# Stick-breaking attention on one Trainium2 core: far mask added by VectorE, off-diagonal sums shortened, value matmuls of two heads interleaved

## The chip, the cores and the metric

The kernel is one program on one core of a Trainium2 chip. It computes two transformer blocks in one launch, over 512 positions of width 1024, in float32 throughout. The metric is the device time of that launch in microseconds (us). The change touches one stage of it, the attention of the last layer.

## The reference, cut to what matters

The last attention is a stick-breaking attention with 16 heads of 64 over 512 positions, causal and strict:

```python
z = einsum('bqhd,bkhd->bhqk', qb, kb) * scale
strict = tk[None, :] < tq[:, None]
log_fail = where(strict, log_sigmoid(-z), 0.0)
between = cumsum(log_fail, axis=-1, reverse=True) - log_fail
a = where(strict, exp(log_sigmoid(z) + between), 0.0)
out = einsum('bhqk,bkhd->bqhd', a, vb)
```

`log_sigmoid(-z)` is minus softplus(z), so the exponent of a pair (query t, key s) is z minus the sum of softplus(z) over the keys from s to t. The masked pairs get a large negative number added to z (the far mask), which makes both softplus and the exponential vanish.

## The kernel before

Scores are kept transposed: keys on the 128 partitions, queries along the free axis. There are four key tiles `kt` of 128, and key tile `kt` needs queries from `kt * 128` on, so it has 512, 384, 256 and 128 columns. Together that is `SB_W` = 1280 columns in three PSUM banks. `SB_AT` says where each tile starts; tiles 0 and 2 begin banks of their own, and tile 3 (at 896) lies behind tile 1 in the second bank. The first 128 columns of each tile are its diagonal block, the only place where the far mask is needed. Two heads alternate between PSUM banks 0 to 2 and 3 to 5; the value outputs of a pair of heads share bank 6 or 7, one head on partitions 0 to 63 and one on 64 to 127.

For each head `h`, in four engines' programs that only semaphores tie together:

- TensorE, `scores(h)`: four matmuls with 64 rows (L1241), 1280 columns in all, then four matmuls of the identity with `k.far` (L1244), 128 columns each, which add the far mask to the diagonal blocks. It may start when the exponential of head `h - 2` has been read out of the same banks (`a.exped`).
- ScalarE: Abs (L1287) of the scores, Exp (L1289), a table load and Ln (L1291), which gives log(1 + exp(-|z|)).
- VectorE (L1309): max(z, 0) plus that, the softplus `k.sp`, 1280 wide. It waits for Ln, and for the sums of the head before.
- TensorE, `sums(h)` (L1254): ten matmuls that subtract the running sums from z in PSUM. Four have `minus_later` (a triangle) as weights and 1280 columns in all; six have `minus_ones` and add the key tiles further on, another 1280 columns.
- ScalarE (L1296): a table load and Exp of the result into `k.tt`.
- TensorE, `values(h)` (L1264): four matmuls with 64 output columns of the array, 1280 columns in all. ScalarE copies the outputs of a pair out (L1300).

The loop is one head deep: in turn `h`, TensorE's order is `scores(h)`, `sums(h - 1)`, `values(h - 2)`, and ScalarE's is Abs, Exp, Ln of `h`, then Exp of `h - 1`, then in odd turns the copy of a pair. Each engine runs its program strictly in that order. After the last head the output projection (L233) follows, then routing and the experts. A float32 matmul instruction leaves two records in the trace, so four of them show as x8.

Of the kernel before, what the change touches and what calls it, by code (L numbers as in the profile page):

```python
# [5 lines left out]
ALU = mybir.AluOpType  # L6
# [15 lines left out]
HEAD = 64  # L22
# [13 lines left out]
DIFF_HEADS, SB_HEADS = 8, 16  # L36
# [24 lines left out]
class Chain:  # L61
# [1159 lines left out]
SB_AT = (0, 512, 1024, 896)  # L1221
# [3 lines left out]
def sb_cols(kt, frm=None):  # L1225

    frm = kt if frm is None else frm
    return slice(SB_AT[kt] + (frm - kt) * P, SB_AT[kt] + (TT - kt) * P)


def sb_scores(k, h):
    return k.ps[:, 3 * (h % 2):3 * (h % 2) + 3, :].rearrange("p b n -> p (b n)")


def sb_tensor(pe, k, a):
    def scores(h):
        if h >= 2:
            pe.wait_ge(a.exped, h - 1)
        r = slice(h % 2 * HEAD, (h % 2 + 1) * HEAD)
        for kt in range(TT):  # L1240
            pe.matmul(sb_scores(k, h)[:, sb_cols(kt)], k.k[r, h // 2, kt * P:(kt + 1) * P],  # L1241
                      k.q[r, h // 2, kt * P:T], start=(kt < TT - 1), stop=False, skip_group_check=True)
        for kt in range(TT):
            mm = pe.matmul(sb_scores(k, h)[:, SB_AT[kt]:SB_AT[kt] + P], k.ident[:, :], k.far,  # L1244
                           start=False, stop=True, skip_group_check=True)
        mm.then_inc(a.scored, 1)

    def sums(h):

        pe.wait_ge(a.softplus, h + 1)  # L1250
        for kt in range(TT):
            for st in range(kt, TT):
                lhs = k.minus_later if st == kt else k.minus_ones
                mm = pe.matmul(sb_scores(k, h)[:, sb_cols(kt, st)], lhs, k.sp[:, sb_cols(st)],  # L1254
                               start=False, stop=True, skip_group_check=True)
        mm.then_inc(a.summed, 1)

    def values(h):
        pe.wait_ge(a.exped, h + 1)
        if h % 2 == 0 and h >= 4:  # L1260
            pe.wait_ge(a.oT_out, h // 2 - 1)
        out = k.ps[h % 2 * HEAD:(h % 2 + 1) * HEAD, 6 + h // 2 % 2, :]
        for kt in range(TT):
            mm = pe.matmul(out[:, kt * P:T], k.v[:, kt, h * HEAD:(h + 1) * HEAD], k.tt[:, h % 2, sb_cols(kt)],  # L1264
                           start=(kt == 0), stop=(kt == TT - 1))
        mm.then_inc(a.valued, 1)

    pe.wait_ge(a.proj_act, QKV_JOBS // 2)
    pe.wait_ge(a.proj_dve, QKV_JOBS // 2)
    for h in range(SB_HEADS + 2):  # L1270
        if h < SB_HEADS:
            scores(h)
        if 1 <= h <= SB_HEADS:
            sums(h - 1)
        if h >= 2:
            values(h - 2)
    pe.wait_ge(a.oT_out, SB_HEADS // 2)


def sb_scalar(act, k, a):  # L1280
    for h in range(SB_HEADS + 2):
        if h < SB_HEADS:

            act.wait_ge(a.scored, h + 1)
            if h:
                act.wait_ge(a.softplus, h)
            act.activation(k.ln[:, :], sb_scores(k, h)[:, 0:SB_W], ACT.Abs).then_inc(a.steps, 1)  # L1287
            act.wait_ge(a.steps, 2 * h + 1)
            act.activation(k.ln[:, :], k.ln[:, :], ACT.Exp, scale=-1.0).then_inc(a.steps, 1)  # L1289
            act.wait_ge(a.steps, 2 * h + 2)  # L1290
            act.activation(k.ln[:, :], k.ln[:, :], ACT.Ln, bias=k.one_col, scale=1.0).then_inc(a.logged, 1)  # L1291
        if 1 <= h <= SB_HEADS:
            act.wait_ge(a.summed, h)
            if h >= 3:
                act.wait_ge(a.valued, h - 2)
            act.activation(k.tt[:, (h - 1) % 2, :], sb_scores(k, h - 1)[:, 0:SB_W], ACT.Exp).then_inc(a.exped, 1)  # L1296
        if h >= 3 and h % 2 == 1:
            pair = (h - 3) // 2
            act.wait_ge(a.valued, 2 * pair + 2)
            act.copy(k.oT[:, pair, :], k.ps[:, 6 + pair % 2, :]).then_inc(a.oT_out, 1)  # L1300


def sb_vector(dve, k, a):

    for h in range(SB_HEADS):
        dve.wait_ge(a.logged, h + 1)
        if h:
            dve.wait_ge(a.summed, h)
        dve.scalar_tensor_tensor(out=k.sp[:, :], in0=sb_scores(k, h)[:, 0:SB_W], scalar=0.0, in1=k.ln[:, :],  # L1309
                                 op0=ALU.max, op1=ALU.add).then_inc(a.softplus, 1)  # L1310

# [407 lines left out]
def place(k, nc, ctx):  # L1719
# [76 lines left out]
    k.dist_i = at(12800, T).bitcast(I32)  # L1796
    k.nmax, k.esum, k.hsmall = at(17408, 2, 4), at(17416, 2, 5), at(17426, 4, TT)
    k.gate_diff, k.gate_diff_b, k.tmp_diff = at(0, D), at(D, D), at(12800, 2, 512)
    k.ln, k.sp, k.tt = at(12288, SB_W), at(13568, SB_W), at(14848, 2, SB_W)
    k.minus_ones, k.minus_later, k.far = at(17408, P), at(17536, P), at(17664, P)  # L1800
    k.gate_sb, k.gate_sb_b, k.tmp_sb = at(12288, D), at(13568, D), at(14848, 2, 512)
# [28 lines left out]
def semaphores(nc, prefix, names):  # L1830
    return [nc.alloc_semaphore(name=prefix + n) for n in names.split()]
# [186 lines left out]
def second_block_layer(nc, k, w, out, l):  # L2018

    s, a, m = Kit(), Kit(), Kit()  # L2020
# [7 lines left out]
    if l == 0:  # L2028
        (a.biased, a.maxed, a.weighed, a.turned, a.turned_out, a.squared, a.var, a.rooted, a.head_normed, a.head_turned) = semaphores(
            nc, "diff_", """biased maxed weighed turned turned_out squared var rooted head_normed head_turned""")  # L2030
    else:
        (a.steps, a.logged, a.softplus, a.summed) = semaphores(
            nc, "sb_", """steps logged softplus summed""")
    k.used[("diff", "sb")[l]] = {"proj": a.proj, "out": a.out}
    (m.router_landed, m.logits, m.g_diff, m.e_diff, m.exps, m.chosen, m.ranked, m.routed, m.scattered, m.x_landed,
     m.x_turned, m.xT_act, m.xT_dve, m.gate_landed, m.up_landed, m.down_landed, m.gated, m.upped, m.downed, m.hidden,
# [22 lines left out]
    with nc.Block() as block:  # L2059
# [151 lines left out]
```

## Time and profile before

| what | us |
| --- | --- |
| median of three runs | 2960.25 |
| the three runs | 2954.14, 2960.25, 2967.46 |
| span of the profiled execution | 2963.8 |
| TensorE matmul busy | 2409.4 (81%) |
| ScalarE busy | 619.3 (21%) |
| VectorE busy | 534.1 (18%) |
| last attention, first scores to the output projection | 2083.4 to 2279.5 |

The profiled execution lies 3.55 us above the median of the runs. The last attention is 196 us of it, 6.6% of the span; there the shares are different from those of the whole, so the rows below are read from that stretch. A timeline row gives the start, the length and the engine of one instruction or a merged group, and in brackets how long the engine sat idle before it and what it then waited for.

### The profile page before, as it was taken

To read this page: it belongs to the slowest core of one execution; us is meant where nothing else is said; L and a number is where in the kernel's file an instruction comes from. 1 tells how busy PE (TensorE), PEld (TensorE's weight loads), DVE (VectorE), ACT (ScalarE), POOL (GpSimd) and SP (SyncE) were. 2 spreads that over 40 slices of the span, in tenths; PEclk is the share of its full clock that TensorE was granted. 3 is DMA by queue.
4 is the path that set the end of the run, shared out by engine and by line. 5 is a ranking of instruction groups with operands and counts; after the bars stand their busy time and mean duration, and the time that the engine had idled before them with its cause. 6 is when DMAs were issued, how large, how long until landed. Compare 5 with 4: busy or idle time off the path is not lost. (4 is left out here: it accounts for less than half of the span.)

```text
span 2963.8 us, 21879 instructions
## 1 busy us (share of the span) xinstructions
PE 2409.4 (81%) x8560; PEld 1103.4 (37%) x8560; DVE 534.1 (18%) x1147; ACT 619.3 (21%) x937; POOL 131.9 (4%) x205
## 2 busy tenths in 40 slices
PE   6988899999997996764888878399899748878773
PEld 3443444444443444441223222244555422222221
DVE  1223532121002016431010010300111211010012
ACT  2213421010001016311121121200564102121121
POOL 2101101000000000001000000100000010000001
PEclk9999789999998998876989999699999868999996
DMA  6245756602221101016999999610200149999994
GB/s 232 72 148 198 254 199 231 253 20 75 103 85 57 57 38 76 15 59 248 427 428 429 428 427 429 256 57 0 114 0 15 59 172 428 428 427 429 428 427 197
DMA packets 126889, 624.34 MB, mean 211 GB/s; under 512 B 13708, under 2 KB 17172, under 8 KB 102252
## 3 DMA queue, kind: packets, MB, share of 16 engines
q1 hardware_dynamic: 102224, 556.35, 46.5%
q0 software_dynamic: 13392, 49.61, 4.5%
q10 hardware_dynamic: 11212, 17.52, 1.6%
q8 instruction: 42, 0.69, 0.1%
q14 instruction: 19, 0.16, 0.0%
HBM read 570.99 MB, written 52.48 MB: 210 GB/s over the span
## 5 line engine op out<-in xcount | busy, mean ns | idle before, releaser
L226 PE MATMUL ps<-hT,ring 128*128 128x512 f32 (+1 forms) x1424 | 619.5, 597 | 9.0 <-DVE hT L181 4.7
L1487 PE MATMUL ps<-ring,arena 128*64 128x512 f32 x2048 | 516.4, 666 | 133.6 <-ACT arena L1515 115.5
L226 PEld LDWEIGHTS ps<-hT,ring 128*128 128x128 f32 (+1 forms) x1424 | 270.3, 190 | 356.4 <-issue 351.8
L1487 PEld LDWEIGHTS ps<-ring,arena 128*64 128x64 f32 x2048 | 160.5, 153 | 467.8 <-issue 385.0
L233 PE MATMUL ps<-ring,hT 128*128 128x512 f32 x640 | 278.6, 596 | 1.5 <-ACT hT L1160 0.8
L1502 PE MATMUL ps<-ring,arena 128*64 128x512 f32 x1024 | 238.7, 620 | 31.3 <-ACT arena L1522 31.3
L233 PEld LDWEIGHTS ps<-ring,hT 128*128 128x128 f32 x640 | 121.8, 191 | 156.9 <-issue 154.8
L948 PE MATMUL ps<-ring,arena 128*128 128x512 f32 x336 | 144.4, 592 | 0.8 <-issue 0.8
L1502 PEld LDWEIGHTS ps<-ring,arena 128*64 128x64 f32 x1024 | 83.0, 142 | 164.9 <-issue 128.1
L1545 DVE TENSOR_TENSOR arena<-ps,arena 128x512 f32<-128x512 f32 x32 | 22.1, 692 | 603.5 <-PE ps L1487 603.5
L189 PE MATMUL ps<-ident,arena 128*128 128x128 f32 x192 | 34.9, 366 | 92.6 <-DVE arena L177 92.6
L948 PEld LDWEIGHTS ps<-ring,arena 128*128 128x128 f32 x336 | 63.8, 190 | 81.5 <-issue 81.5
L1477 PE MATMUL ps<-ident,arena 128*128 128x128 f32 x256 | 38.7, 296 | 66.1 <-DMA arena<-token_slots 66.1
L1254 PE MATMUL ps<-arena 128*128 128x128 f32 (+3 forms) x320 | 79.1, 405 | 4.7 <-DVE arena L1309 4.7
L1044 ACT ACTIVATE arena<-ps 128x512 f32<-128x512 f32 x24 | 14.3, 597 | 307.0 <-PE ps L226 201.9
L1548 DVE COPY arena<-ps 128x512 f32<-128x512 f32 x32 | 22.1, 692 | 300.1 <-PE ps L1502 300.1
L1522 ACT COPY arena<-ps 128x512 f32<-128x512 f32 x32 | 18.8, 586 | 270.6 <-PE ps L1492 270.6
L1050 DVE TENSOR_SCALAR arena<-ps 128x512 f32<-128x512 f32 x24 | 16.6, 691 | 318.5 <-PE ps L226 214.2
L1520 ACT ACTIVATE arena<-ps 128x512 f32<-128x512 f32 x32 | 19.1, 597 | 257.8 <-PE ps L1487 257.8
L1525 ACT COPY arena<-ps 128x512 f32<-128x512 f32 x32 | 18.8, 586 | 254.0 <-PE ps L1502 254.0
L189 PEld LDWEIGHTS ps<-ident,arena 128*128 128x128 f32 x192 | 33.8, 214 | 96.8 <-DVE arena L177 91.8
L971 ACT COPY arena<-ps 128x512 f32<-128x512 f32 x21 | 12.3, 587 | 259.0 <-PE ps L226 259.0
(329 smaller groups left out, 2060.3 us busy)
## 6 DMA issues: line engine op xcount, KB each, us to landing
ring<-in_expert_w_gate SPq DMA_DIRECT2D x64, 2048.0 KB, 16.6
ring<-in_expert_w_down SPq DMA_DIRECT2D x64, 2048.0 KB, 19.7
ring<-in_expert_w_up SPq DMA_DIRECT2D x64, 2048.0 KB, 19.6
ring<-in_ada_w SPq DMA_DIRECT2D x24, 2048.0 KB, 12.9
arena<-token_slots SPq DMA_DIRECT2D x32, 512.0 KB, 22.8
output_slots<-arena ACTq DMA_DIRECT2D x32, 512.0 KB, 10.2
token_slots<-arena POOLq DMA_DIRECT2D x1, 12288.0 KB, 40.5
output_slots<-arena POOLq DMA_DIRECT2D x1, 12288.0 KB, 77.5
```

The source lines that it names most:

```text
L189: mm = pe.transpose(k.ps[:, c, tt * P:(tt + 1) * P], k.xn[:, tt, c::KD], k.ident[:, :])
L226: mm = pe.matmul(out, w[:, c, cols], x[:, c, :], start=(c == 0), stop=(c == chunks - 1))
L233: mm = pe.matmul(out, x[:, c, tt * P:(tt + 1) * P], w[:, c, :], start=(c == 0), stop=(c == chunks - 1))
L948: mm = pe.matmul(k.ps[:, 4 * half + tt, :], k.actT[:, c0 + c, tt * P:(tt + 1) * P], w[:, c, :], start=(c0 + c == 0), stop=(c0 + c == FT - 1))
L1254: mm = pe.matmul(sb_scores(k, h)[:, sb_cols(kt, st)], lhs, k.sp[:, sb_cols(st)], start=False, stop=True, skip_group_check=True)
L1477: mm = pe.transpose(k.ps[:, c // 4, c % 4 * P:(c % 4 + 1) * P], k.xg[:, c::KD], k.ident[:, :])
L1487: mm = pe.matmul(k.ps[slots, 2 + kind, :], k.xT[:, c, slots], w[:, c, :], start=(c == 0), stop=(c == KD - 1))
L1502: mm = pe.matmul(k.ps[slots, 5 + half, :], k.hTt[:, c, slots], w[:, c, half * 512:(half + 1) * 512], start=(c == 0), stop=(c == KH - 1))
L1520: act.activation(k.sg[:, :], k.ps[:, 2, :], ACT.Silu).then_inc(m.silu, 1)
L1522: act.copy(k.hTt[:, :, :].rearrange("p c s -> p (c s)"), k.ps[:, 4, :]).then_inc(m.hT_out, 1)
L1545: dve.tensor_tensor(k.hid[:, :], k.ps[:, 3, :], k.sg[:, :], ALU.mult).then_inc(m.hidden, 1)
L1548: dve.tensor_copy(k.ys[:, 512:1024], k.ps[:, 6, :]).then_inc(m.y_dve, 1)
```

## The change

Three things change in the attention of the last layer.

1. The four identity matmuls that added the far mask are gone. VectorE adds it in PSUM with two instructions for each head (`mark(h)`: three blocks of 128 in one, then the last block). ScalarE's Abs now waits for these (`a.marked`). `mark(h + 1)` stands behind the softplus of head `h` in VectorE's program.
2. `sums` has nine matmuls in place of ten and 2048 columns in place of 2560: VectorE first adds off-diagonal tiles of `k.sp` into `k.spc` (three additions of 128 columns each), and the last two matmuls read that, behind a wait for `a.carried`.
3. `values` is called once for a pair of heads, with the matmuls of the two heads alternating, and stands ahead of `sums` in odd turns; even turns have none.

```diff
         for kt in range(TT):
-            for st in range(kt, TT):
-                lhs = k.minus_later if st == kt else k.minus_ones
-                mm = pe.matmul(sb_scores(k, h)[:, sb_cols(kt, st)], lhs, k.sp[:, sb_cols(st)],
-                               start=False, stop=True, skip_group_check=True)
-        mm.then_inc(a.summed, 1)
+            pe.matmul(z[:, sb_cols(kt)], k.minus_later, k.sp[:, sb_cols(kt)], start=False, stop=True, skip_group_check=True)
+        for kt in range(TT - 1):
+            pe.matmul(z[:, sb_block(kt, kt + 1)], k.minus_ones, k.sp[:, sb_block(kt + 1, kt + 1)],
+                      start=False, stop=True, skip_group_check=True)
+        pe.wait_ge(a.carried, 3 * h + 3)
+        pe.matmul(z[:, sb_block(0, 2, 2)], k.minus_ones, k.spc[:, 0:2 * P], start=False, stop=True, skip_group_check=True)
+        pe.matmul(z[:, sb_block(1, 3)], k.minus_ones, k.spc[:, 2 * P:3 * P], start=False, stop=True, skip_group_check=True)\
+            .then_inc(a.summed, 1)
...
+    def values(pair):
+        pe.wait_ge(a.exped, 2 * pair + 2)
+        if pair >= 2:
+            pe.wait_ge(a.oT_out, pair - 1)
         for kt in range(TT):
-            mm = pe.matmul(out[:, kt * P:T], k.v[:, kt, h * HEAD:(h + 1) * HEAD], k.tt[:, h % 2, sb_cols(kt)],
-                           start=(kt == 0), stop=(kt == TT - 1))
+            for n in range(2):
+                h = 2 * pair + n
+                mm = pe.matmul(k.ps[n * HEAD:(n + 1) * HEAD, 6 + pair % 2, kt * P:T], k.v[:, kt, h * HEAD:(h + 1) * HEAD],
+                               k.tt[:, n, sb_cols(kt)], start=(kt == 0), stop=(kt == TT - 1))
...
+    def mark(h):
+        dve.wait_ge(a.scored, h + 1)
+        diagonal = k.ps[:, 3 * (h % 2):3 * (h % 2) + 3, 0:P]
+        dve.tensor_tensor(diagonal, diagonal, k.far.unsqueeze(1).to_broadcast([P, TT - 1, P]), ALU.add).then_inc(a.marked, 1)
+        last = sb_scores(k, h)[:, sb_block(TT - 1, TT - 1)]
+        dve.tensor_tensor(last, last, k.far, ALU.add).then_inc(a.marked, 1)
...
+        dve.wait_ge(a.softplus, h + 1)
+        dve.tensor_tensor(k.spc[:, 2 * P:3 * P], k.sp[:, sb_block(2, 3)], k.sp[:, sb_block(3, 3)], ALU.add).then_inc(a.carried, 1)
+        dve.tensor_tensor(k.spc[:, 0:P], k.sp[:, sb_block(1, 2)], k.sp[:, sb_block(2, 2)], ALU.add).then_inc(a.carried, 1)
+        dve.wait_ge(a.carried, 3 * h + 1)
+        dve.tensor_tensor(k.spc[:, P:2 * P], k.sp[:, sb_block(1, 3)], k.spc[:, 2 * P:3 * P], ALU.add).then_inc(a.carried, 1)
+        if h + 1 < SB_HEADS:
+            mark(h + 1)
```

On TensorE, before, one turn of the steady loop (the mask matmuls L1244, the ten sums L1254, the values of one head L1264, the next scores L1241) reads so:

```order
L1244 MATMUL ps<-arena,ident 128x128 x4
L1254 MATMUL ps<-arena 128x512
L1254 MATMUL ps<-arena 128x384
L1254 MATMUL ps<-arena 128x256
L1254 MATMUL ps<-arena 128x128
...
L1264 MATMUL ps<-arena 64x512
L1264 MATMUL ps<-arena 64x384
L1264 MATMUL ps<-arena 64x256
L1264 MATMUL ps<-arena 64x128
L1241 MATMUL ps<-arena 128x512
```

On TensorE, of the changed kernel, an odd turn from the end of its scores (L1246) to the start of the next, even turn: L1271 is the values of a pair, L1255 and L1257 the sums from `k.sp`, L1260 and L1261 those from `k.spc`.

```order
L1246 MATMUL ps<-arena 128x128
L1271 MATMUL ps<-arena 64x512 x2
L1271 MATMUL ps<-arena 64x384 x2
L1271 MATMUL ps<-arena 64x256 x2
L1271 MATMUL ps<-arena 64x128 x2
L1255 MATMUL ps<-arena 128x512
L1255 MATMUL ps<-arena 128x384
L1255 MATMUL ps<-arena 128x256
L1255 MATMUL ps<-arena 128x128
L1257 MATMUL ps<-arena 128x128 x3
L1260 MATMUL ps<-normw,arena 128x256
L1261 MATMUL ps<-normw,arena 128x128
```

The mask matmuls have left the queue, the values moved from behind the sums to ahead of them, and in the even turn that follows nothing stands between the scores and the sums, nor behind the sums until the next scores.

On VectorE, before, the whole stage is one kind of instruction (L1309, the softplus), between the last copies of the projections (L1050) and the output projection's products and sums:

```order
L1050 TENSOR_SCALAR arena<-ps 128x512 x12
L1309 SCALAR_TENSOR_TENSOR arena<-ps,arena 128x1280 x16
L1069 TENSOR_TENSOR arena<-ps,arena 128x512
L1071 TENSOR_TENSOR x<-x,arena 128x512
L1069 TENSOR_TENSOR arena<-ps,arena 128x512
```

On VectorE, of the changed kernel, the first heads of the stage read so (L1315 and L1317 are `mark`, L1325 the softplus, L1328, L1329 and L1331 the additions into `k.spc`):

```order
L1315 TENSOR_TENSOR ps<-ps,arena 128x3x128
L1317 TENSOR_TENSOR ps<-ps,arena 128x128
L1325 SCALAR_TENSOR_TENSOR arena<-ps,arena 128x1280
L1328 TENSOR_TENSOR normw<-arena 128x128
L1329 TENSOR_TENSOR normw<-arena 128x128
L1331 TENSOR_TENSOR normw<-arena,normw 128x128
L1315 TENSOR_TENSOR ps<-ps,arena 128x3x128
L1317 TENSOR_TENSOR ps<-ps,arena 128x128
L1325 SCALAR_TENSOR_TENSOR arena<-ps,arena 128x1280
```

The mask of head 0 comes ahead of its softplus; from then on the mask of head `h + 1`, for which Abs of that head waits, stands behind the softplus and the three additions of head `h`.

ScalarE's instructions and their order are unchanged but for what they wait for.

## Rows read from the trace of the kernel before

**Rows 1.** Stage by windows: length, then busy us (instructions) per engine, granted clock, DMA share, GB/s.

```profile
2083.00:2280.00 197.00, 176.33 (x705) 114.97 (x706) 24.15 (x17) 128.06 (x105) 1.17 (x2) 0.92 0.12 48
```

**Rows 2.** Waits in 14 turns of the loop: us in total, times, longest.

```profile
ACT arena L1287 <- PE ps L1244: 54.6, 14, 5.1
PE ps L1241 <- ACT arena L1296: 14.9, 13, 1.9
```

**Rows 3.** Timeline of one turn at the full clock: start, us, engine, what.

```profile
2180.25 4.50 PE L1254 MATMUL ps<-arena 128*128 128x512 f32 x20
...
2180.45 1.24 ACT L1287 ACTIVATE arena<-ps 128x1280 f32<-128x1280 f32 x1 [2.85 <-PE ps L1244]
...
2184.68 2.37 PE L1264 MATMUL ps<-arena 128*64 128x512 f32 x8
...
2185.69 1.49 DVE L1309 SCALAR_TENSOR_TENSOR arena<-ps,arena 128x1280 f32<-128x1280 f32 x1 [9.42 <-ACT arena L1291]
...
2186.97 1.24 ACT L1296 ACTIVATE arena<-ps 128x1280 f32<-128x1280 f32 x1
...
2188.26 2.42 PE L1241 MATMUL ps<-arena 64*128 64x512 f32 x8 [1.22 <-ACT arena L1296]
...
2190.61 1.16 PE L1244 MATMUL ps<-arena,ident 128*128 128x128 f32 x8
...
2191.81 1.24 ACT L1287 ACTIVATE arena<-ps 128x1280 f32<-128x1280 f32 x1 [3.60 <-PE ps L1244]
```

**Rows 4.** Timeline of a turn at the low clock, and windows around such a fall.

```profile
2163.53 2.97 PE L1241 MATMUL ps<-arena 64*128 64x512 f32 x8 [1.22 <-ACT arena L1296]
...
2168.30 6.38 PE L1254 MATMUL ps<-arena 128*128 128x512 f32 x20
...
2115.00:2117.00 2.00, 1.48 (x4) 0.86 (x5) 0.00 (x0) 0.47 (x1) 0.00 (x0) 1.00 0.00 0
2117.00:2119.00 2.00, 2.00 (x8) 1.52 (x7) 0.00 (x0) 0.00 (x0) 0.00 (x0) 0.62 0.00 0
```

**Rows 5.** Timeline, ScalarE: Abs of heads 2 and 15.

```profile
2107.71 1.24 ACT L1287 ACTIVATE arena<-ps 128x1280 f32<-128x1280 f32 x1 [3.60 <-PE ps L1244]
...
2263.27 1.24 ACT L1287 ACTIVATE arena<-ps 128x1280 f32<-128x1280 f32 x1 [4.65 <-PE ps L1244]
```

**Rows 6.** Timeline and window of the first two heads.

```profile
2095.02 7.24 PE L1254 MATMUL ps<-arena 128*128 128x512 f32 x20 [4.67 <-DVE arena L1309]
...
2095.07 1.24 ACT L1287 ACTIVATE arena<-ps 128x1280 f32<-128x1280 f32 x1 [1.62 <-DVE arena L1309]
...
2104.16 2.42 PE L1241 MATMUL ps<-arena 64*128 64x512 f32 x8 [1.90 <-ACT arena L1296]
...
2095.00:2097.00 2.00, 1.98 (x3) 0.95 (x4) 0.00 (x0) 1.92 (x2) 0.00 (x0) 0.50 1.01 434
```

**Rows 7.** The first attention: TensorE timeline and windows.

```profile
1141.39 0.90 PE L1099 MATMUL ps<-ident,arena 128*128 128x128 f32 x3 [5.49 <-DVE arena L1189]
...
1138.00:1140.00 2.00, 0.00 (x0) 0.00 (x0) 1.97 (x7) 0.98 (x1) 0.00 (x0) 0.50 0.00 0
1142.00:1144.00 2.00, 2.00 (x12) 1.67 (x10) 1.38 (x4) 1.25 (x5) 0.00 (x0) 0.50 0.00 0
```

**Rows 8.** Timeline, TensorE: expert matmuls on half the columns alternating; projection matmuls.

```profile
1417.55 7.09 PE L1502 MATMUL ps<-ring,arena 128*64 128x512 f32 x32 [0.68 <-ACT arena L1522]
...
999.68 12.61 PE L226 MATMUL ps<-hT,ring 128*128 128x512 f32 x29
```

**Rows 9.** Groups by line and form, VectorE: busy us, mean ns, idle before.

```profile
L1545 DVE TENSOR_TENSOR arena<-ps,arena 128x512 f32<-128x512 f32 x32 | 22.1, 692 | 603.5 <-PE ps L1487 603.5
...
L1347 DVE TENSOR_TENSOR arena<-arena 128x128 f32<-128x128 f32 x4 | 1.2, 292 | 0.1
```

**Rows 10.** Timeline of the end of the stage.

```profile
2274.89 3.93 PE L1264 MATMUL ps<-arena 128*64 128x512 f32 x16
...
2279.49 20.87 PE L233 MATMUL ps<-ring,hT 128*128 128x512 f32 x48 [0.68 <-ACT hT L1300]
```

More of the change, by code:

```diff
@@ L1228, in sb_cols, with sb_block @@
     return slice(SB_AT[kt] + (frm - kt) * P, SB_AT[kt] + (TT - kt) * P)
+def sb_block(kt, q, n=1):
+    return slice(SB_AT[kt] + (q - kt) * P, SB_AT[kt] + (q - kt + n) * P)
 def sb_scores(k, h):
@@ L1240, in scores @@
         for kt in range(TT):
[L1241 to L1244, printed above, removed]
-                           start=False, stop=True, skip_group_check=True)
+            mm = pe.matmul(sb_scores(k, h)[:, sb_cols(kt)], k.k[r, h // 2, kt * P:(kt + 1) * P],
+                           k.q[r, h // 2, kt * P:T], start=(kt < TT - 1), stop=True, skip_group_check=True)
         mm.then_inc(a.scored, 1)
@@ L1250, in sums @@
         pe.wait_ge(a.softplus, h + 1)
+        z = sb_scores(k, h)
         for kt in range(TT):
-            for st in range(kt, TT):
-                lhs = k.minus_later if st == kt else k.minus_ones
-                mm = pe.matmul(sb_scores(k, h)[:, sb_cols(kt, st)], lhs, k.sp[:, sb_cols(st)],
-                               start=False, stop=True, skip_group_check=True)
-        mm.then_inc(a.summed, 1)
[L1258 to L1262, printed above, removed]
+            pe.matmul(z[:, sb_cols(kt)], k.minus_later, k.sp[:, sb_cols(kt)], start=False, stop=True, skip_group_check=True)
[10 more added lines that the diff above has]
+            pe.wait_ge(a.oT_out, pair - 1)
         for kt in range(TT):
-            mm = pe.matmul(out[:, kt * P:T], k.v[:, kt, h * HEAD:(h + 1) * HEAD], k.tt[:, h % 2, sb_cols(kt)],
-                           start=(kt == 0), stop=(kt == TT - 1))
+            for n in range(2):
+                h = 2 * pair + n
+                mm = pe.matmul(k.ps[n * HEAD:(n + 1) * HEAD, 6 + pair % 2, kt * P:T], k.v[:, kt, h * HEAD:(h + 1) * HEAD],
+                               k.tt[:, n, sb_cols(kt)], start=(kt == 0), stop=(kt == TT - 1))
         mm.then_inc(a.valued, 1)
@@ L1272, in sb_tensor @@
             scores(h)
+        if h >= 3 and h % 2:
+            values((h - 3) // 2)
         if 1 <= h <= SB_HEADS:
             sums(h - 1)
-        if h >= 2:
-            values(h - 2)
     pe.wait_ge(a.oT_out, SB_HEADS // 2)
@@ L1282, in sb_scalar @@
         if h < SB_HEADS:
-            act.wait_ge(a.scored, h + 1)
+            act.wait_ge(a.marked, 2 * h + 2)
             if h:
@@ L1294, in sb_scalar @@
             if h >= 3:
-                act.wait_ge(a.valued, h - 2)
+                act.wait_ge(a.valued, (h - 1) // 2)
             act.activation(k.tt[:, (h - 1) % 2, :], sb_scores(k, h - 1)[:, 0:SB_W], ACT.Exp).then_inc(a.exped, 1)
@@ L1298, in sb_scalar @@
             pair = (h - 3) // 2
-            act.wait_ge(a.valued, 2 * pair + 2)
+            act.wait_ge(a.valued, pair + 1)
             act.copy(k.oT[:, pair, :], k.ps[:, 6 + pair % 2, :]).then_inc(a.oT_out, 1)
 def sb_vector(dve, k, a):
+    def mark(h):
[4 more added lines that the diff above has]
+        dve.tensor_tensor(last, last, k.far, ALU.add).then_inc(a.marked, 1)
+    dve.wait_ge(k.s.later_ready, 2)
+    mark(0)
     for h in range(SB_HEADS):
@@ L1798, in place @@
     k.gate_diff, k.gate_diff_b, k.tmp_diff = at(0, D), at(D, D), at(12800, 2, 512)
+    k.spc = k.normw[:, 0:3 * P]
     k.ln, k.sp, k.tt = at(12288, SB_W), at(13568, SB_W), at(14848, 2, SB_W)
@@ L2031, in second_block_layer @@
     else:
-        (a.steps, a.logged, a.softplus, a.summed) = semaphores(
-            nc, "sb_", """steps logged softplus summed""")
+        (a.steps, a.logged, a.softplus, a.marked, a.carried, a.summed) = semaphores(
+            nc, "sb_", """steps logged softplus marked carried summed""")
     k.used[("diff", "sb")[l]] = {"proj": a.proj, "out": a.out}
```

## The prediction

> **What bounds the stage now.** I read the windows of the stage first, then the waits, then the timeline of one turn, because the page's shares are averages over stages with other limits. In the stage [rows 1] TensorE is busy 176 of 197 us, ScalarE 128, VectorE 24: that looks like a TensorE bound. The waits say otherwise. In 14 turns Abs waited 54.6 us for the mask matmuls, and the scores waited 13 times, 14.9 us, for ScalarE's last Exp [rows 2]. The two engines form a ring, and the timeline shows it closed [rows 3]: Abs of one head at 2180.45; Abs, Exp, table load, Ln, table load, Exp run on without a gap until 2186.97 + 1.24 = 2188.21, which is 7.76 us; the next scores start 0.05 later, at 2188.26; the mask matmuls follow; the next Abs starts at 2191.81, 3.55 us after the scores. Turn: 11.36 us = 7.76 + 0.05 + 3.55. The sums (4.43 us from 2180.25 to 2184.68) and the values (2.37) run beside ScalarE's 7.76 us. They end 1.22 us before the scores may start, so at the full clock they are hidden.
>
> From Abs of head 2 to Abs of head 15 there are 13 turns in 155.56 us [rows 5], 11.97 each, 0.61 above the full-clock turn. The rest is TensorE's clock. Between 2115 and 2117 TensorE is busy 1.48 of 2 us at a granted clock of 1.00, and in the next 2 us it is at 0.62, though busy all the time; the waits before scores are where the clock falls [rows 4]. Where it falls, the scores and the mask take 4.77 us to the start of the sums (2163.53 to 2168.30), and Abs starts 0.2 after that, so 4.97 in place of 3.55: a turn costs 1.4 more, and somewhat more where sums and values are late too (sums 6.38 in place of 4.50). At 0.61 a turn this happens in about every second one.
>
> **The mask on VectorE (part 1).** Removed from the ring: the mask matmuls, at the full clock 3.55 - 2.42 - 0.04 = 1.09 us of it [rows 3]. Put in their place: one addition over 3 x 128 and one over 128, from PSUM to PSUM, which no row shows. The nearest rows are an addition of 512 from PSUM, 692 ns, and one of 128, 292 ns [rows 9]; the line through them gives 559 for 384. So 0.85, with two hand-overs and a gap 0.95; at worst two of the 512-wide kind, 1.4; at best, if only the streaming counts (400 ns for 384 wider), 0.6. I take 0.95: the ring gets 0.15 shorter, a turn 11.2. VectorE has room: softplus begins 5.24 us after Abs (2185.69), lasts 1.49, the three additions take 3 x 0.3 = 0.9, so it is free 7.65 us after Abs, while the next scores end 10.2 after it. Only in the first turns does the queue matter (below).
>
> **The shorter sums (part 2).** 2048 columns for 2560: 4.43 x 0.8 = 3.55 us. Off the ring at the full clock: worth nothing there by itself. The wait for the additions comes after seven matmuls (about 2.9 us) and the additions take 0.9, so it holds nothing up.
>
> **The values in pairs (part 3).** Alternating matmuls on two halves of the columns run side by side in the expert stage: 32 records of 512 columns in 7.09 us, 0.22 each, against 0.43 each for full-width ones [rows 8]. A pair would take 2.2 us if perfect and 4.5 if not at all; the widths fall from 512 to 128 and each matmul has two records, so I take 2.65. That is hidden too: in an odd turn 2.65 + 3.55 = 6.2 us stand behind the scores, and the Exp that needs the sums comes 0.95 + 6.5 = 7.45 us behind them.
>
> **What TensorE does with the time.** All three parts empty TensorE in a ring whose length hardly changes. It had 1.22 us of idle time a turn. In an even turn it will have 11.2 - 2.35 - 3.55 = 5.3 us in one piece, ahead of the scores on which the ring waits; in an odd turn 11.2 - 2.35 - 6.2 = 2.6 us. What such a gap does stands in two places. Ahead of the first sums TensorE was idle 4.67 us, and it then ran them at a granted clock of 0.50, 1.2 GHz: 7.24 us [rows 6]. In the first attention it was idle 5.49 us; the clock was 0.50 before the gap was over and still 0.50 through 2 us of full work [rows 7]. So the scores of every odd turn run at half clock: their 2.13 us of streaming (1280 columns, at the rate of 0.43 for 512 columns and two records for each matmul) doubles, +2.1 on the ring, or +1.9 where the clock returns within them. The values behind them are slow in part, about +1, and still covered (7.2 against 7.45). In even turns the gap is 2.6 less what the slow turn took, about 2; that is more than the 1.22 after which the clock falls in every second turn now, so I put between half (0.6) and all (1.4) of a fall there: 1.0.
>
> The Trainium skill, page TensorE: Matmul & The Clock Gate, Part 1, says that the default state is throttled and that activity releases the throttle. It speaks against this change. By that rule the sum is the one below; without it the ring alone would give the first rival's time. The rows just named agree with it.
>
> **The sum, against the profiled execution (2963.8 us).**
> Steady turns: an odd one 11.2 + 2.0 = 13.2, an even one 11.2 + 1.0 = 12.2, mean 12.7; 13 x (12.7 - 11.97) = **+9.5**.
> Beginning: Abs of head 1 started at 2095.07, straight after softplus. Now it is behind the three additions and its own mask, 0.9 + 0.95: +1.85, less 0.15 for head 0. The first sums are short, so ahead of the scores of head 2 (2104.16 before, after 1.90 idle [rows 6]) there is a gap of over 4 us, and these scores run slow: +2.1, less 0.15. **+3.6** (+1.6 if the clock stays).
> End: before, 2263.27 to 2279.49, 16.2 us from Abs of head 15 to the output projection [rows 5, 10]. After: Ln ends 5.2 after Abs, softplus 1.5, sums 3.6 with their drain, Exp 1.3, the pair of values 2.8, the copy 0.65, small hand-overs 0.2: 15.25. **-1.0**. At half clock the last of these would cost up to 2 more.
> Together +12.1: 2975.9 for such an execution. The profiled one lies 3.55 above the median of its runs, so **2972 us** for the median. Nothing behind the stage hides this: its weights have landed, and the output projection starts when the last copy is done. The forecast's own spread, from 0.6 to 1.4 for the even turns, 0.6 to 1.4 for the mask and 0 to 2 at the end, is 2964 to 2983.
>
> **Rivals.**
> *The clock holds.* If the idle pieces fall so that it keeps 2.4 GHz, the ring alone counts: 13 x (11.2 - 11.97) = -10, beginning +1.6, end -1: -9.4, 2951. For it: in about half of the turns the clock did hold over an idle piece of over 1 us, and values of two heads at once keep more of the array busy. Against: both rows with gaps of about 5 us. 0.13.
> *Half clock in both turns and late sums.* If an odd turn is slow from scores to sums, these end at 5.1 + 7.1 = 12.2 us behind the scores against 7.45 needed, and Exp is late by 4.7; it decides where the clock stays low for well over 7 us of work after a gap. After the first gap it was low for some 2 x (7.24 - 4.50) = 5.5 us [rows 3, 6]. With the even turns slow as well (+2.1) and one odd turn in three late like this (+1.6 on average) the mean turn is 11.2 + 2.1 + 0.8 = 14.1: 13 x 2.1 = +28, ends +5: 2993. 0.2.
> *The values don't run side by side.* Pairs of unequal records, each matmul's two in a row, may take turns. Then a pair is 4.5 us, 8.05 behind the scores at the full clock, 0.6 late in an odd turn; with half of the values at half clock as well 6.5 + 3.55 = 10.05, 2.6 late. 7 x 2.6 = +18 on the forecast: 2990. 0.04.
> A mask as dear as two 512-wide additions adds 13 x 0.45 = 6 to any of these; the ranges hold it.
>
> **Chances.** Forecast 0.63, clock holds 0.13, half clock throughout 0.2, values apart 0.04. A measurement of this kernel tells about 0.5% (15 us) from no change. The forecast lies 12 above the median with a spread of some 7, so 0.41 of its 0.63 is within that and 0.22 is slower; the clock rival gives 0.03 faster and 0.10 same; the others slower but for 0.01. Sum: faster 0.03, same 0.52, slower 0.45. The range takes the forecast whole, half of the way to the first rival and the second rival with half its weight: 2955 to 2993.
>
> **What would show it.** Right: turns (Abs to Abs) that alternate near 13 and 12 us; over 5 us idle ahead of every second scores, and 0.50 in the windows over them; scores of 4.5 us there; a mask of 0.85 us; pairs of values of 2.6 to 2.8 us at the full clock; sums of 3.6. The mean granted clock of the stage falls from 0.92 to about 0.75. Wrong: turns near 11.2 throughout (first rival); Exp that waits for the sums for several us (second and third). The forecast would also be wrong if VectorE's instructions on PSUM were far from the line through the two rows.

## The result, and the profile after

The changed kernel takes 2972.74 us (median of 10 runs, 2969.55 to 2981.45), the kernel before 2960.97 (10 runs, 2954.14 to 2967.46): a ratio of 1.004, 95% interval [1.0029, 1.0051]. It is slower by about 12 us, 0.4%.

The profiled execution has a span of 2968.3 us against 2963.8. The last attention, from its first scores to the output projection, takes 2076.27 to 2282.28 = 206.0 us against 196.1, so 9.9 more; the rest of the program was 5.4 shorter in this one execution, which is within what executions differ by (13 us between the runs before). The 12 us between the medians have an interval of 9 to 15, and the 9.9 us of the stage lie inside it. The stage by windows (columns as in [rows 1]), then the windows in which the granted clock falls ahead of one head's scores and through them:

```profile
2083.00:2280.00 197.00, 153.05 (x516) 91.20 (x518) 46.37 (x94) 123.96 (x102) 1.17 (x2) 0.76 0.07 30
2184.00:2186.00 2.00, 0.00 (x0) 0.00 (x0) 1.63 (x4) 1.95 (x2) 0.00 (x0) 0.97 0.00 0
2186.00:2188.00 2.00, 1.99 (x3) 0.95 (x4) 0.00 (x0) 0.00 (x0) 0.00 (x0) 0.50 0.00 0
```

TensorE's busy time went from 176 to 153 us, VectorE's from 24 to 46, and the mean granted clock from 0.92 to 0.76 [rows 1]. Between 2186 and 2188 TensorE is busy all the time, at 1.2 GHz. The waits in the 14 turns:

```profile
DVE arena L1325 <- PE ps L1261: 61.1, 9, 7.7
ACT arena L1294 <- DVE ps L1317: 60.5, 14, 5.5
...
PE ps L1246 <- ACT arena L1303: 36.3, 14, 5.0
...
ACT arena L1303 <- PE ps L1261: 3.8, 4, 1.1
```

TensorE waited 36.3 us ahead of the scores, where it had waited 14.9 [rows 2]. Abs waited 60.5 where it had waited 54.6. And four times Exp (L1303) waited for the sums (L1261), 3.8 us in all. An even turn and the odd turn behind it, then the next Abs (L1294 Abs, L1261 the end of the sums, L1303 the last Exp, L1246 scores, L1271 values of a pair, L1315 and L1317 the mask on VectorE):

```profile
2178.20 1.24 ACT L1294 ACTIVATE arena<-ps 128x1280 f32<-128x1280 f32 x1 [2.83 <-DVE ps L1317]
...
2180.66 0.38 PE L1261 MATMUL ps<-normw,arena 128*128 128x128 f32 x2
...
2184.72 1.24 ACT L1303 ACTIVATE arena<-ps 128x1280 f32<-128x1280 f32 x1
...
2186.01 4.63 PE L1246 MATMUL ps<-arena 64*128 64x512 f32 x8 [4.97 <-ACT arena L1303]
...
2190.57 3.41 PE L1271 MATMUL ps<-arena 128*64 128x512 f32 x16
2190.68 0.57 DVE L1315 TENSOR_TENSOR ps<-ps,arena 128x384 f32<-128x384 f32 x1 [5.02 <-PE ps L1246]
2191.16 0.29 DVE L1317 TENSOR_TENSOR ps<-ps,arena 128x128 f32<-128x128 f32 x1
2191.48 1.24 ACT L1294 ACTIVATE arena<-ps 128x1280 f32<-128x1280 f32 x1 [5.52 <-DVE ps L1317]
...
2193.92 2.42 PE L1255 MATMUL ps<-arena 128*128 128x512 f32 x8
...
2199.29 2.42 PE L1246 MATMUL ps<-arena 64*128 64x512 f32 x8 [1.63 <-ACT arena L1303]
...
2202.55 1.24 ACT L1294 ACTIVATE arena<-ps 128x1280 f32<-128x1280 f32 x1 [2.83 <-DVE ps L1317]
```

The sums of the even turn are over at 2181.04, the scores of the odd turn start at 2186.01 after 4.97 idle us and take 4.63 instead of 2.42 [rows 3]. That turn, Abs at 2178.20 to Abs at 2191.48, lasts 13.28 us. The next, with 1.63 idle ahead of its scores and the clock up, lasts 11.07.

From Abs of head 2 to Abs of head 15 there are 162.47 us, 12.50 a turn, against 11.97 [rows 5]. The seven turns into odd heads last 12.95 on average, the six into even heads 11.97. The mask is faster than forecast: from its start at 2190.68 to Abs at 2191.48 are 0.80 us, against 0.95. The end of the stage:

```profile
2266.06 1.24 ACT L1294 ACTIVATE arena<-ps 128x1280 f32<-128x1280 f32 x1 [5.35 <-DVE ps L1317]
...
2272.61 1.49 DVE L1325 SCALAR_TENSOR_TENSOR arena<-ps,arena 128x1280 f32<-128x1280 f32 x1 [6.58 <-PE ps L1261]
...
2282.28 18.29 PE L233 MATMUL ps<-ring,hT 128*128 128x512 f32 x42 [0.69 <-ACT hT L1307]
```

The last softplus waits for the sums of head 14 (L1261), which a slow odd turn has made late.

### The profile page after: what moved, and what is told of

Read it like the earlier page. It is cut to its first block and busy times, and to the rows that moved or that the text cites. A ratio compares the mean times of both kernels' runs of the same rounds, so it can differ in the third digit from the quotient of the medians.

```text
span 2968.3 us, 21640 instructions
## 1 busy us (share of the span) xinstructions
PE 2386.7 (80%) x8400; PEld 1079.1 (36%) x8400; DVE 557.6 (19%) x1227; ACT 618.9 (21%) x937; POOL 131.5 (4%) x205
## 5 line engine op out<-in xcount | busy, mean ns | idle before, releaser
L1246 PE MATMUL ps<-arena 64*128 64x384 f32 (+3 forms) x128 | 54.9, 596 | 37.2 <-ACT arena L1303 36.3
L1050 DVE TENSOR_SCALAR arena<-ps 128x512 f32<-128x512 f32 x24 | 16.6, 692 | 318.6 <-PE ps L226 214.3
## 6 DMA issues: line engine op xcount, KB each, us to landing
arena<-token_slots SPq DMA_DIRECT2D x32, 512.0 KB, 22.9
```

Of the source, the lines that this page charges most:

```text
L1246: mm = pe.matmul(sb_scores(k, h)[:, sb_cols(kt)], k.k[r, h // 2, kt * P:(kt + 1) * P], k.q[r, h // 2, kt * P:T], start=(kt < TT - 1), stop ...
```

## The experiments

All times are medians, with the ratio to the runs of the kernel before on the same chip (their medians are 2959.7 to 2961.0, so rows compare across series to within about 1 us). "Turn" is the mean from Abs of head 2 to Abs of head 15 in the profiled execution, "stage" is from the first scores to the output projection, "clock" the mean granted clock of that stretch. These three come from one execution each; it took 8 us more than the median in e11_fill_even3, 8 less in e5_mask, and lay within 5 of it in the others.

| kernel | us | ratio, 95% interval | turn | stage | clock |
| --- | --- | --- | --- | --- | --- |
| before | 2960 | | 11.97 | 196.1 | 0.92 |
| changed | 2972.7 | 1.0029 to 1.0051 | 12.50 | 206.0 | 0.77 |
| e1_fill: changed, gaps filled | 2949.9 | 0.9942 to 0.9973 | 11.14 | 184.9 | 0.99 |
| e2_fill_even: only the long gaps filled | 2973.6 | 1.0025 to 1.0051 | 12.73 | 207.8 | 0.83 |
| e11_fill_even3: the same, fewer matmuls | 2964.3 | 0.9998 to 1.0020 | 11.58 | 192.8 | 0.85 |
| e3_before_fill: before, gaps filled | 2955.1 | 0.9968 to 0.9992 | 11.36 | 188.5 | 1.00 |
| e4_apart: changed, values head by head | 2985.2 | 1.0059 to 1.0099 | 13.04 | 217.6 | 0.81 |
| e5_mask: before with part 1 | 2959.5 | 0.9986 to 1.0011 | 11.45 | 189.1 | 0.89 |
| e6_values: before with part 3 | 2986.5 | 1.0067 to 1.0099 | 13.72 | 221.2 | 0.82 |
| e7_sums: before with part 2 | 2962.5 | 0.9998 to 1.0027 | 11.96 | 197.8 | 0.91 |
| e8_mask_fill: part 1, gaps filled | 2952.4 | 0.9959 to 0.9982 | 11.09 | 185.4 | 1.00 |
| e9_mask_twice: e1 with a second mask | 2963.7 | 1.0005 to 1.0023 | 11.86 | 196.0 | 0.98 |
| e10_mask_sums: changed without part 3 | 2960.8 | 0.9997 to 1.0014 | 11.60 | 193.2 | 0.85 |

### Is it the clock? Gaps filled (e1_fill)

`fill` issues idle matmuls, whose result nobody reads, into a value bank that is free. Behind the scores of head 1, behind the first sums and behind the sums of every turn they take the place of idle time.

```diff
+    def fill(n, bank):
+        for _ in range(n):
+            pe.matmul(k.ps[:, bank, :], k.minus_ones, k.q[:, 0, :], start=True, stop=True)
...
+        if h == 1:
+            fill(7, 7)
...
+        if 1 <= h < SB_HEADS:
+            p = (h - 3) // 2
+            if p >= 1:
+                pe.wait_ge(a.oT_out, p)
+            fill(7 if h == 1 else (5, 2)[h % 2], 6 + (p + 1) % 2)
```

> The changed kernel with idle matmuls added on TensorE, whose result nobody reads: full-width matmuls of 512 columns (0.86 us each) into the value bank that is free, 7 behind the scores of head 1, 7 behind the first sums, then 5 behind the sums of every even turn and 2 behind those of every odd turn, so that the gaps ahead of the scores shrink from about 5 and 2 us to under 1.2. Nothing else changes. Theory (the clock falls in the gaps): granted clock of the stage near 1.00, every turn (Abs to Abs) near the 11.07 us of the changed kernel's few undisturbed turns, 13 x (12.50 - 11.07) = 18.6 us less in the steady turns and 2 to 3 less at both ends: 2951 us, 9 under the kernel before. Rival (the hand-over to VectorE and its queue are what made the turns longer, the low clock is a bystander): no change, 2973. Rival (work added on the busiest engine is late for the scores): over 2973.

Measured: 2949.9, 22.9 us less than the changed kernel and 10 less than the one before. The stage and two Abs one turn apart:

```profile
2081.30:2266.20 184.90, 171.20 (x671) 96.49 (x671) 47.12 (x96) 127.95 (x105) 1.18 (x2) 0.99 0.12 50
```

```profile
2139.65 1.24 ACT L1305 ACTIVATE arena<-ps 128x1280 f32<-128x1280 f32 x1 [3.31 <-DVE ps L1328]
...
2150.72 1.24 ACT L1305 ACTIVATE arena<-ps 128x1280 f32<-128x1280 f32 x1 [2.83 <-DVE ps L1328]
```

Eleven of the 13 turns last 11.07 or 11.08. The two others, 11.32 and 11.71, lie around one fall of the clock that came all the same: in the first the scores took 2.68, in the second the five idle matmuls, late behind slow sums, held the scores back. With more work on TensorE and nothing else changed the loss is gone, so neither VectorE's mask nor its queue made the turns long. The clock did.

### Only the long gaps filled (e2_fill_even)

```diff
-            fill(7 if h == 1 else (5, 2)[h % 2], 6 + (p + 1) % 2)
+            fill(0 if h == 1 else (5, 0)[h % 2], 6 + (p + 1) % 2)
```

(and no matmuls behind the scores of head 1)

> The same idle matmuls only behind the sums of even turns (5 each), none in odd turns and none at the start. Theory: the slow scores of odd turns go (12.95 to 11.1, 7 turns, -13 us), the even turns, behind a gap of 2 to 3 us, stay as they are (12.0) or get slower by up to 0.5: total 2958 to 2963. If the gap of 5 us is not what matters, no change: 2973.

Measured: 2973.6, no gain. The expectation missed. On TensorE and ScalarE (L1312 is the last Exp, L1277 the idle matmuls), from the scores of an odd head on:

```profile
2145.31 2.42 PE L1246 MATMUL ps<-arena 64*128 64x512 f32 x8
...
2156.47 4.60 PE L1246 MATMUL ps<-arena 64*128 64x512 f32 x8 [2.76 <-ACT arena L1312]
...
2167.05 4.46 PE L1277 MATMUL ps<-arena 128*128 128x512 f32 x10
...
2168.43 1.24 ACT L1312 ACTIVATE arena<-ps 128x1280 f32<-128x1280 f32 x1
...
2171.43 2.42 PE L1246 MATMUL ps<-arena 64*128 64x512 f32 x8
```

The scores of odd heads, up to which the idle matmuls now run without a gap, are fast again (2.42 in all seven). The total is the one named for the case that the long gap doesn't matter, but the rows show another reason: two things took the gain. With fast scores in the odd turn the gap ahead of the next scores is the full 2.76 us (2.67 once), and there the clock falls: 3.96 to 4.60 behind every such gap of this trace, and turns into even heads of 13.11 on average. In the changed kernel that gap had been small only because the turn ahead of it was slow. And the sums behind these slow scores end late, so that five idle matmuls run until 2171.43, while Exp is over at 2169.67: the next scores are 1.8 late through my own filling. The turns into odd heads last 12.41 on average though their scores are fast; the 1.3 over 11.07 is this lateness.

### The same with three idle matmuls (e11_fill_even3)

```diff
-            fill(0 if h == 1 else (5, 0)[h % 2], 6 + (p + 1) % 2)
+            fill(0 if h == 1 else (3, 0)[h % 2], 6 + (p + 1) % 2)
```

> As the kernel filled only behind the sums of even turns, but with 3 idle matmuls instead of 5. With 5, the sums of an even turn, slow themselves after the fall ahead of their scores, ended late and the idle matmuls held the next scores back by up to 1.8 us (Exp was over at 2169.67, the scores started at 2171.43). With 3 (2.6 us) they fit into the 2.7 us that are left there. Theory: scores of odd heads fast and on time, turns into odd heads 11.1 to 11.4; scores of even heads slow behind the full gap of 2.8 us, turns of 13.0 to 13.3; mean 12.1 to 12.3 against 12.50, and the end 1 us shorter: 2965 to 2969. Rival (filling the long gap gives nothing of itself, or the clock does not hold over what is left of it): 2972 and more.

Measured: 2964.3, 8.4 less than the changed kernel. The turns into odd heads last 11.07 to 11.32, the seven of them 11.13 on average in place of 12.95. Those into even heads last 12.10, with everything from 11.13 to 13.35. Two of their scores:

```profile
2161.09 4.60 PE L1246 MATMUL ps<-arena 64*128 64x512 f32 x8 [2.76 <-ACT arena L1312]
...
2185.75 2.39 PE L1246 MATMUL ps<-arena 64*128 64x512 f32 x8 [2.76 <-ACT arena L1312]
...
2188.07 4.12 PE L1255 MATMUL ps<-arena 128*128 128x512 f32 x8
```

So the long gap, half filled, gives back about two thirds of what the two gaps cost in the steady turns (11.58 a turn, against 12.50 and 11.14) of this execution, one of the two longest of its twelve; the medians are 8.4 apart. The expected 2965 to 2969 was missed by under 1, the 13.0 to 13.3 for even heads by more. The rows show why. The clock fell behind both gaps of 2.76 us, but at different moments. In the first turn the granted clock is 0.50 in the windows from 2161 on, and the scores are slow, on which the ring waits. In the second it is 1.00 until 2188 and 0.57 from 2188 to 2190: the scores are over, the fall hits the first sums (4.12 in place of 2.42), these are hidden behind ScalarE, and the turn lasts 11.13. What a fall costs depends on which matmuls it hits.

### The kernel before, gaps filled (e3_before_fill)

The same `fill` in the kernel before: 5 and 5 at the start, then `fill(1, ...)` behind the values of each turn.

> The kernel before (no part of the change) with idle matmuls of 512 columns: 5 behind the scores of head 1, 5 behind the first sums, and one (0.86 us) behind the values of each turn, where 1.22 us were idle. Theory: the falls of the clock in about every second turn go, turns of 11.36 in place of 11.97, 13 x 0.61 = 8 us less and up to 1 less at the start: 2952 us. With the first kernel of this call (the changed one, filled) it gives what the change is worth with the clock held: 0.3 us a turn, 4 to 5 us in all. Rival (a gap of 1.22 us does not matter, the falls have another cause): 2961, or slower if the added matmul is late.

Measured: 2955.1. Abs of heads 2 and 15:

```profile
2106.80 1.24 ACT L1298 ACTIVATE arena<-ps 128x1280 f32<-128x1280 f32 x1 [3.60 <-PE ps L1244]
...
2254.48 1.24 ACT L1298 ACTIVATE arena<-ps 128x1280 f32<-128x1280 f32 x1 [3.60 <-PE ps L1244]
```

147.68 us for 13 turns, 11.36 each, and each single one is 11.36. The stage lost 7.6 us, as expected (8); the whole program 5, where 8 had been expected. So the falls of the kernel before did hang on its 1.22 us of idle time a turn. With the clock held on both sides, the change is worth 2955.1 - 2949.9 = 5.2 us between the medians, in the stage 188.5 - 184.9 = 3.6.

### Do alternating values run side by side? (e4_apart)

```diff
-        for kt in range(TT):
-            for n in range(2):
+        for n in range(2):
+            for kt in range(TT):
```

> The changed kernel with the value matmuls of a pair issued head after head instead of alternating: same work, same place in the queue. If the halves of the array run side by side only when they alternate, a pair takes 4.5 us at the full clock in place of 2.4, the sums of an odd turn end 8 us or more behind the scores against 7.45 needed, later still at the low clock: 7 odd turns longer by 1 to 5 us each, 2980 to 3008. If alternating gives nothing: 2973.

Measured: 2985.2, 12.4 more than the changed kernel. An odd turn on TensorE and the Exp that waits for its sums:

```profile
2171.45 4.63 PE L1246 MATMUL ps<-arena 64*128 64x512 f32 x8 [4.97 <-ACT arena L1303]
...
2176.01 6.42 PE L1271 MATMUL ps<-arena 128*64 128x512 f32 x16
...
2186.14 1.24 ACT L1303 ACTIVATE arena<-ps 128x1280 f32<-128x1280 f32 x1 [2.35 <-PE ps L1261]
...
2298.48 3.93 PE L1271 MATMUL ps<-arena 128*64 128x512 f32 x16 [1.33 <-ACT arena L1303]
```

and the last pair of the changed kernel:

```profile
2279.22 2.38 PE L1271 MATMUL ps<-arena 128*64 128x512 f32 x16 [1.32 <-ACT arena L1303]
```

The values of a pair take 6.42 us, part of them at half clock, where the alternating ones took 3.41; Exp comes 2.35 late. The last pair of each is the clean comparison, for the granted clock is 1.00 in both places (2298 to 2302 and 2280 to 2282): 3.93 head after head, 2.38 alternating. So part 3 does what it says.

### Each part alone (e5_mask, e7_sums, e6_values)

Each is the kernel before with one part of the change, taken over word for word.

> The kernel before with only part 1: the mask on VectorE, the old ten sums and the values head by head. With the clock held the turn would be 11.07 us; TensorE's gap ahead of the scores grows from 1.22 to 1.9 us. Theory (each us taken from TensorE comes back as a lower clock): falls at least as often as before, each dearer by none of the mask, so turns between 11.6 and 12.2 on average against 11.97: 2955 to 2966, the 0.29 us a turn kept or just given back. Rival (the clock falls only after gaps of several us): 11.07 + 0.61 = 11.7, less 0.3 a turn: 2957.

> The kernel before with only part 2: VectorE's three additions and the shorter sums, mask matmuls and values by head as before. Gap 1.22 + 0.88 = 2.1 us ahead of every scores. Theory: falls more often than before, up to every turn (+1.4 where full): mean turn 12.0 to 12.7 against 11.97, 2961 to 2971. Rival (shorter sums help wherever they were late at the low clock): 2955 to 2960.

> The kernel before with only part 3: values of a pair alternating, ahead of the sums in odd turns, mask matmuls and ten sums as before. Gap ahead of the scores: 1.2 us after odd turns, 3.6 after even ones. Theory: the gap of 3.6 costs the scores and the mask of every odd turn full half clock, +2.1 and +1.0 us; and in an odd turn the sums end 1.0 + 2.4 + 4.5 = 7.9 us behind the scores against 7.5 needed, later still at half clock (+1 to 2): mean turn 13.0 to 13.6, 13 x 1.3 = +17: 2972 to 2984. This is the part that makes the change slow. Rival: the three parts share the loss, each alone +4: 2965.

Measured: 2959.5, 2962.5 and 2986.5, against 2960. Parts 1 and 2 alone can't be told from no change, within what was expected of them. (The profiled execution of e5_mask took 2951.3, 8 us under its own median; its turn and stage are those of one short execution.) These two say little by themselves: what was expected of the theory and of the rival overlapped for part 1, and the 2962.5 of part 2 lies at the low end of the theory's range. Part 3 alone costs 26 us, more than the 12 to 24 expected, and more than the whole change; the rival, three parts that share the loss, is out. Its odd turn:

```profile
2166.74 4.63 PE L1246 MATMUL ps<-arena 64*128 64x512 f32 x8 [3.52 <-ACT arena L1302]
...
2171.30 2.07 PE L1249 MATMUL ps<-arena,ident 128*128 128x128 f32 x8
...
2176.77 4.60 PE L1259 MATMUL ps<-arena 128*128 128x512 f32 x20
...
2181.41 1.24 ACT L1302 ACTIVATE arena<-ps 128x1280 f32<-128x1280 f32 x1 [1.47 <-PE ps L1259]
```

After a gap of 3.52 us both the scores and the mask matmuls run at half clock (4.63 and 2.07), the sums end late, and Exp waits 1.47 us for them. This repeats without exception: turns of 14.49 and 12.83. The first is the 11.36 of the full clock with 2.2 for the scores and 0.9 for the mask matmuls, the second the same 11.36 with the 1.47 of the late Exp. My sum for it had 13.0 to 13.6 a turn, the mean is 13.72. In the whole change the mask on VectorE and the shorter sums take away a part of that: the mask is not slowed by TensorE's clock, and the sums are back in time.

### Part 1 with the clock held (e8_mask_fill)

Part 1 alone, with `fill(6, ...)` twice at the start and `fill(2, ...)` behind the values of each turn.

> Part 1 alone with idle matmuls (two of 512 columns a turn, six each at the two places of the start), old sums and values. Theory: with the clock held the ring alone counts and of the change only the mask is in it, so the same turn as the filled kernel with all three parts, 11.07, and the same time, 2950; parts 2 and 3 are worth nothing once the clock is held. Rival (shorter sums and paired values are worth something of their own): 2953 or more.

Measured: 2952.4, turns of 11.09. The turn is that of e1_fill but for 0.02, the stage 0.5 longer. The medians differ by 2.5, where the intervals overlap. So of the three parts it is the mask that shortens the ring; parts 2 and 3 are worth nothing in the steady turns with the clock held. They show at the ends alone: from Abs of head 15 to the output projection there are 16.78 us here and 14.94 in e1_fill, from the first scores to Abs of head 2 24.37 here and 25.10 there.

### The price of VectorE's place in the ring (e9_mask_twice)

e1_fill with this, one idle matmul more in each turn, and Abs waiting for three marks a head in place of two:

```diff
         dve.tensor_tensor(diagonal, diagonal, k.far.unsqueeze(1).to_broadcast([P, TT - 1, P]), ALU.add).then_inc(a.marked, 1)
+        dve.wait_ge(a.marked, 3 * h + 1)
+        dve.tensor_tensor(diagonal, diagonal, k.far.unsqueeze(1).to_broadcast([P, TT - 1, P]), ALU.add).then_inc(a.marked, 1)
```

> The filled kernel with all three parts, and the three-block mask addition done twice (masked pairs get twice the large negative number, which changes nothing in the result), the second behind the first; one idle matmul more a turn (6 and 3), so that the gaps stay small. It prices VectorE's place in the ring: the instruction lasts 0.57 us, with the wait on the first about 0.6. If the mask is in the ring, each turn is longer by that much, 11.07 to 11.67, 15 turns: +9 us on 2949.9, 2958 to 2960. If VectorE's mask lies beside something else, 2950.

Measured: 2963.7, 13.8 more than e1_fill. One turn:

```profile
2166.20 0.57 DVE L1326 TENSOR_TENSOR ps<-ps,arena 128x384 f32<-128x384 f32 x1 [2.81 <-PE ps L1246]
...
2166.80 0.57 DVE L1328 TENSOR_TENSOR ps<-ps,arena 128x384 f32<-128x384 f32 x1
...
2167.28 0.29 DVE L1330 TENSOR_TENSOR ps<-ps,arena 128x128 f32<-128x128 f32 x1
...
2167.60 1.24 ACT L1305 ACTIVATE arena<-ps 128x1280 f32<-128x1280 f32 x1 [3.91 <-DVE ps L1330]
...
2179.27 1.24 ACT L1305 ACTIVATE arena<-ps 128x1280 f32<-128x1280 f32 x1 [3.43 <-DVE ps L1330]
```

Eleven of the 13 turns last 11.67, 0.60 more than 11.07, as expected: the mask stands in the ring with its whole length. Two others last 12.88 and 12.87. In both the scores, behind a gap of 0.69 us, are still fast (2.42), the granted clock is 0.50 behind them (2202 to 2204 and 2250 to 2252), the first sums take 4.12, and the six idle matmuls behind the sums end late: they hold the next scores back by 1.2. With the start (1.8 longer) that makes 11 us in the stage. So the price was right by turn, and the expected total, 2958 to 2960, was some 5 too low.

### The change without part 3 (e10_mask_sums)

> The changed kernel with part 3 taken back: mask on VectorE and shorter sums, values head by head behind the sums of every turn. Gap ahead of every scores 11.07 - 8.3 = 2.8 us at the full clock. Theory: what makes the change slow is that pairing empties the even turns; without it the low clock comes after a gap of up to 2.8 us, in some turns, as in the kernels with part 1 or 2 alone (11.45 and 11.96 a turn): mean turn 11.6 to 12.4, total 2955 to 2967, faster than the whole change by 6 to 18. Rival (any gap of 2.8 us brings full falls, as in the kernel filled only in even turns, where every such gap did): turns of 13.2, 2980.

Measured: 2960.8, 12 us less than the whole change. So the whole loss of the change comes with part 3, given the other two. The mask and part of the sums are off TensorE as in the changed kernel, but every turn has its values. In the trace the gaps ahead of the scores of even heads are 2.67 or 2.68 (4.11 ahead of head 2), those ahead of odd heads 1.48 at most, since slow matmuls of the turn before fill them in part. The turns into odd heads all keep 11.07, and those into even heads lie between 11.07 and 13.3. Two even heads, the second with its first sums:

```profile
2172.84 4.56 PE L1246 MATMUL ps<-arena 64*128 64x512 f32 x8 [2.68 <-ACT arena L1302]
...
2221.48 2.42 PE L1246 MATMUL ps<-arena 64*128 64x512 f32 x8 [2.67 <-ACT arena L1302]
2223.83 4.12 PE L1255 MATMUL ps<-arena 128*128 128x512 f32 x8
```

The first turn lasts 13.21, the second 11.07. Again the fall came behind both gaps, once on the scores and once on sums that are hidden (the granted clock is 1.00 from 2221 to 2223 and 0.50 from 2225 to 2227).

## Why the prediction was right, and where it was off

The forecast was 2972 and the cause it named, slow scores behind the gaps that the change opens, is what e1_fill shows. By its steps:

- **The ring.** Forecast 11.2 us a turn at the full clock, measured 11.07. The mask was put at 0.95 and took 0.80: 566 ns for the 3 x 128 form and 290 for the last block, as the line through the two rows had it, but the second starts before the first is over (2190.68, 2191.16, Abs at 2191.48).
- **Odd turns.** Forecast 13.2, measured 12.95. The scores of all seven run slow, five of them nearly throughout (4.46 to 4.63), two in part (3.62 and 3.64), and what they take over 2.42 is what the turn lasts over 11.07, to 0.01 us. The idle piece ahead of them was put at 5.3 us; it was 4.97 twice, behind fast even turns, and 2.28 to 3.53 else, because a slow even turn lengthens its own sums. The length by itself did not set the harm: behind 2.28 to 2.67 us it was 2.0 to 2.2, as behind 4.97, and behind the two of 3.5 it was 1.2.
- **Even turns.** Forecast 12.2, measured 11.97, but for another reason in part. The step "1.0 for falls in even turns" is the one that failed: their scores took 2.42 to 3.05, a cost of 0.3 on average. The rest, 3.8 / 6 = 0.6 a turn, is Exp that waited for the sums. I had called the slow values covered (7.2 against 7.45); in four odd turns the values and sums were slow for longer than the 1 us that I had put there, and Exp was late by 0.8 to 1.1. It is a small form of the second rival. So the 1.0 for even turns came out near the measured 0.9 by luck.
- **The sum of the steady turns.** +9.5 forecast, 13 x 0.53 = +6.9 measured; 1.7 of the difference is the ring, shorter by 0.13 a turn than forecast.
- **Beginning.** +3.6 forecast, 27.32 - 24.28 = +3.0 measured, from the first scores to Abs of head 2. The scores of head 2 took 4.63 after 3.76 idle. VectorE's additions and mask together delayed Abs of head 1 by 1.35 (2.94 us from the start of softplus, against 1.59), not 1.85: the three additions start at 2087.62, 2087.83 and 2088.03 and the mask at 2088.23, every 0.2 us, though each lasts 0.29.
- **End.** -1.0 forecast, 0.0 measured. The sum put softplus straight after Ln; it waited 1.3 us for the late sums of head 14. Where the clock is held (e1_fill) the end takes 14.94 us, 1.3 under before, so what the sum left out is that the last turn is an odd one, with late sums.
- **Total.** +12.1 forecast, +9.9 in the stage of the profiled execution and +11.8 between the medians. The steady turns were put 2.6 too high, the beginning 0.6 too high and the end 1.0 too low. The forecast is the median before plus 12.1, and 12.1 against 11.8 is closer than its terms were; that is luck. For a profiled execution it gave 2975.9, and the one taken had a span of 2968.3, since the rest of the program was 5.4 shorter in it. The mechanism and the size of the main term, the slow scores of odd turns (+2.0 forecast, 1.9 measured), are no luck.

**The rivals.** The clock that holds was priced at 2951; e1_fill, which makes it hold, gives 2949.9. Half clock throughout and late sums (2993) came only in the small form just named, but e6_values is that case in the kernel with the old mask and sums: 2986.5, with Exp 1.47 late. Values that take turns were priced at 2990 with 4.5 us a pair; e4_apart, where they stand head after head, gives 2985.2 and 3.93 us a pair at the full clock.

The Trainium skill, page TensorE: Matmul & The Clock Gate, Part 1, has the throttled state as the default and activity as what lifts it. The traces of this case agree: the granted clock goes to 0.50 around idle pieces (0.50 from 2186 to 2188, behind 4.97 idle us), and work that nobody needs makes the kernel faster (2949.9 against 2972.7 in e1_fill, 2955.1 against 2960 in e3_before_fill).

**What stays open:** what sets the moment of a fall. Behind gaps of one length it came ahead of the scores, within them or behind them (the 2.76 us of e2_fill_even and e11_fill_even3), and gaps of 1.33 us were followed by scores of 2.42 in all twelve cases of e4_apart and e6_values, but of 2.62 to 3.05 in the four of the changed kernel. A few falls came after gaps of under 1 us (e1_fill, e9_mask_twice). No experiment here varied this by itself.

## What to carry to other kernels

Before taking work off TensorE, ask whether it bounds the stage or stands in a ring with others. In a ring, what is taken off beside the ring turns into idle time, and this kernel paid for idle time ahead of the scores with their speed. If a part of the work must leave, try to let it leave evenly: moving two heads' values into one turn left the other empty and cost 12 us on top of the other two parts, 26 alone. Where nothing useful was at hand to fill a gap, matmuls that nobody reads did it here, as long as they ended before the wait did (e2_fill_even). e1_fill, 10 us faster than the kernel before, has the lowest median of all versions; e8_mask_fill (2952.4) is not told apart from it.

## What the runs showed that was not expected

- In the kernel before, six of the eight steady gaps of 1.22 us ended in scores that were slow in part (2.56 to 2.97 in place of 2.42), while none of 0.93 or less did; closing them by one matmul each removed every fall (e3_before_fill).
- A fall of the clock is not dear by itself. In e11_fill_even3 and e10_mask_sums one came just behind the scores, the first sums took 4.12 us in place of 2.42, and the turns lasted 11.13 and 11.07; on the scores it cost up to 2.3.
- Alternating value matmuls of unequal widths lose nothing: a pair takes 2.38 us, about what one head alone takes (2.37 [rows 3]), while the same pair head after head takes 3.93 (e4_apart).
- VectorE's additions within PSUM lie on the line through the two rows that had other operands, 692 ns for 512 columns out of PSUM and 292 for 128 columns outside it [rows 9]: 566 ns for 3 x 128 in three banks (the line gives 559), 290 for 128.
